# mLSTM of a two-layer trunk: own buffers for gate and second direction, its last products in other slots, unread products in another wait of PE

## The reference

```
u = layer_norm(x) * (1 + scale) + shift          # scale, shift, gate = silu(c) @ w_mod + b_mod
parts = split(u @ w_in)                          # q, k, v, z of branches A, B, C; B's o and gates; g_merge
# branch B, mLSTM, chunks of 128 tokens, forward and backward (d = 0, 1), 4 heads
s   = (q k^T) * exp(D - m)                       # "ST": scores, times decays
num = s v + w_inter * (C q)                      # "ND": numerator and, in column 129, denominator
den = sum(s) + w_inter * (n q)
h   = num / max(|den|, exp(-m))
C   = wc * C + (ws v)^T k                        # "CS": the state's update; "CX": the last state
y   = sigmoid(o) * (h_forward + h_backward)
merged += sigmoid(g) * ((y * silu(z)) @ w_branch)
x   = layer_norm(alpha * x + gate * (merged @ w_out)) * ln_g + ln_b
```

## Time and profile before

| | us |
|---|---|
| median of 3 runs | 1595.09 (1593.09 to 1595.38) |
| the profiled execution | 1593.39 |
| its span, first to last instruction | 1591.6 |
| PE busy in it | 1529.0 |
| mLSTM, from `scores(0)` to the gate projection, layer 0 / layer 1 | 644.09 to 666.75 / 1412.76 to 1437.35 |

### The profile page before, as it was taken

One profiled execution on the slowest core, in us unless ns is written; L12 is line 12 of the kernel. 1 busy time (PEld: TensorE's weight loads), 2 busy tenths in 40 slices (PEclk: granted clock), 3 DMA queues, 4 the chain that ended last, 5 costly groups with the idle time before them and its releaser, 6 DMA issues.

```text
span 1591.6 us, 22536 instructions
## 1 busy us (share of the span) xinstructions
PE 1529.0 (96%) x9059; PEld 1251.7 (79%) x9059; DVE 741.8 (47%) x1442; ACT 470.4 (30%) x1095; POOL 631.2 (40%) x504
## 2 busy tenths in 40 slices
PE   5999999999899999899999999999989999999997
PEld 4898788886688887788878977889758888777886
DVE  4496710646423332622497584125670136262256
ACT  1146710155410123411034485012571003232010
POOL 2561045600355353155772400555104554413562
PEclk9999999999999999999999999999999999999999
DMA  9220012327122222025440100222401221211421
GB/s 346 84 83 28 1 53 79 100 69 244 57 66 80 66 67 60 27 67 185 110 132 28 60 25 14 67 80 80 132 6 53 80 79 54 67 47 40 172 79 66
DMA packets 76135, 128.71 MB, mean 81 GB/s; under 512 B 16188, under 2 KB 20736, under 8 KB 76032
## 3 DMA queue, kind: packets, MB, share of 16 engines
q1 hardware_dynamic: 73792, 121.24, 24.7%
q10 hardware_dynamic: 2240, 6.03, 1.0%
HBM read 120.96 MB, written 6.30 MB: 80 GB/s over the span
## 4 chain that ended last, share of the span: by engine, by line
PE 79%; DVE 9%; POOL 3%; issue 3%; ACT 2%; DMA 2%; SPq 1%; POOLq 0%; DVEq 0%; ACTq 0%
PE pb L983 54%; PE pb L1126 5%; PE pb L1255 4%; PE pb L1008 2%; PE pb L1206 2%; PE pb L1169 2%; PE pb L931 2%; PE pb L1177 1%; PE pb L1299 1%; DMA stage<-in_w_mod 1%; DVE ks L2059 1%; PE pb L1436 1%; POOL slot_T L833 1%; DMA raw<-in_w_mod 1%; ACT pr L1704 1%
## 5 line engine op out<-in xcount | busy, mean ns | idle before, releaser
L983 PE MATMUL pb<-wsp,act_T 128*128 128x512 f32 x3060 | 714.5, 391 | 3.8 <-POOL wsp L833 2.1
L983 PEld LDWEIGHTS pb<-wsp,act_T 128*128 128x128 f32 x3060 | 570.9, 188 | 127.5 <-issue 7.8
L830 POOL CAST wsp<-raw 128x1024 fp32r<-128x1024 f32 x128 | 136.3, 1065 | 833.6 <-PE pb L983 664.6
L833 POOL TENSOR_TENSOR wsp<-raw,wsp 128x512 fp32r<-128x512 f32 x268 | 359.6, 1363 | 10.2
L983 PE MATMUL pb<-wsp,yT 128*128 128x512 f32 x720 | 165.7, 390 | 0.0
L983 PEld LDWEIGHTS pb<-wsp,yT 128*128 128x128 f32 x720 | 135.0, 188 | 27.9
L2516 DVE SCALAR_TENSOR_TENSOR mt<-tg,pb 128x512 f32<-128x512 f32 x40 | 27.4, 686 | 230.6 <-PE pb L983 229.7
L1854 ACT ACTIVATE tg<-pb 128x512 f32<-128x512 f32 x60 | 35.9, 599 | 289.6 <-PE pb L983 289.6
L1704 ACT ACTIVATE pr<-pb,nm 128x640 f32<-128x640 f32 (+2 forms) x128 | 91.3, 713 | 4.8 <-DVE nm L2200 4.8
L1206 PE MATMUL pb<-ident,pr 128*128 128x128 f32 x480 | 74.6, 277 | 7.2 <-ACT pT L1739 6.8
L2230 DVE TENSOR_SCALAR pr<-pr,rden 128x640 f32<-128x640 f32 (+2 forms) x128 | 69.8, 545 | 4.5
(11 more groups left out here) (281 smaller groups left out, 1961.7 us busy)
## 6 DMA issues: line engine op xcount, KB each, us to landing
raw<-in_w_in SPq DMA_DIRECT2D x112, 512.0 KB, 3.6
raw<-in_w_mod SPq DMA_DIRECT2D x32, 512.0 KB, 4.7
raw<-in_w_branch SPq DMA_DIRECT2D x24, 512.0 KB, 3.7
raw<-in_w_out SPq DMA_DIRECT2D x16, 512.0 KB, 3.7
stage<-in_w_mod SPq DMA_DIRECT2D x12, 512.0 KB, 11.7
raw<-in_w_in SPq DMA_DIRECT2D x16, 256.0 KB, 5.0
xh<-in_x_sample SPq DMA_DIRECT2D x6, 512.0 KB, 6.6
out<-xh ACTq DMA_DIRECT2D x5, 512.0 KB, 3.0
```

Source lines behind the costliest of these rows:

```text
L830: pool.tensor_copy(hi, raw[:, p % 3, :, 0:width]).then_inc(raw_hi, 1)
L833: ins = pool.tensor_tensor(lo[:, j, :], raw[:, p % 3, j, 0:width], hi[:, j, :].bitcast(F32), ALU.subtract)
L983: mm = pe.matmul(dst, lhs(a, k, t), w[:, wa, j, 0:width], start=(k == 0 and n == 0), stop=(i == count - 1 and j == 1 and n == 2))
```

## The change

Six edits. (1) At the start 6 unread products after i = 0 take the place of 8 after i = 1. (2) `ztmp` moves to addresses of its own, and the two waits of `decayed` on `zo` go; `finish` waits for `zo` instead. (3) `gate_zo` of tile 4 moves behind both denominators of chunk 0. (4) `t4` has two buffers, taken by turns; ACT's direction 1 waits for the read two chunks back. (5) The state updates CS 3, 4, 5 move from z's steps 17, 18, 19 to 16, 17, 18, so `scores(0)` follows z's last tile at once. (6) `hs` is turned in two groups: chunks 0 to 2 after part 0 of the gate projection, 3 and 4 after part 1.

```
-                     ("CS", (11, 13, 15, 17, 18, 19))):
+                     ("CS", (11, 13, 15, 16, 17, 18))):
...
-        t4 = at("t4", [P, HALF], F32, y_at + 18432)
...
-        ztmp = at("ztmp", [P, 2, HALF], F32, arena + 41056)
+        ztmp = at("ztmp", [P, 2, HALF], F32, arena + 79360)
+        t4 = at("t4", [P, 2, HALF], F32, arena + 83456)
...
+                        if i == 0:
+                            keep_busy(6)
                         if i == 1:
-                            keep_busy(8)
                             pe.wait_ge(xn_ready[0], T)
...
-                    if (i, t) == (0, T - 1):
-                        for c in range(T):
+                    if i < 2 and t == T - 1:
+                        for c in ((0, 1, 2), (3, 4))[i]:
...
-                            if d == 1 and c:
-                                act.wait_ge(t4_used[l], c)
+                            if d == 1 and c > 1:
+                                act.wait_ge(t4_used[l], c - 1)
                             for h in range(MH):
-                                dst = (hs[:, t, :], t4)[d][:, tile_cols(h)]
+                                dst = (hs[:, t, :], t4[:, c % 2, :])[d][:, tile_cols(h)]
...
-                        elif n != 1:
-                            dve.wait_ge(zo_ready[l], T - 1 if n == 0 else T)
...
-                        dve.tensor_tensor(hs[:, t, :], hs[:, t, :], t4[:, :], ALU.add).then_inc(t4_used[l], 1)
+                        dve.tensor_tensor(hs[:, t, :], hs[:, t, :], t4[:, c % 2, :], ALU.add).then_inc(t4_used[l], 1)
                         dve.wait_ge(t4_used[l], c + 1)
+                        dve.wait_ge(zo_ready[l], T if t == LT else t + 1)
...
                     for d in range(2):
                         decayed(0, d)
-                    gate_zo(T - 1)
...
                         if c:
                             finish(c - 1)
+                        else:
+                            gate_zo(T - 1)
```

## The result

| | before | after |
|---|---|---|
| median | 1594.38 us (1593.09 to 1595.38, 4 runs) | 1582.51 us (1581.72 to 1584.38, 4 runs) |
| the profiled execution, its span | 1593.39, 1591.6 | 1582.43, 1580.6 |
| start of the first projection | 34.14 | 32.16 |
| `scores(0)` to the gate projection, layer 0 / 1 | 22.66 / 24.59 | 20.12 / 20.11 |

The ratio is 0.9932, with a 95% interval of 0.992 to 0.9945: faster by 0.7%. The forecast was 1584.2 with a range of 1579.5 to 1589.0. Both profiled executions lie near their medians, so the 11.0 us between the spans can be followed along PE. How far after is ahead of before: 1.98 at the first projection, still 1.97 at `scores(0)` of layer 0, 4.51 at the gate projection behind its loop, 5.48 at the product with `yT`, 5.60 at `scores(0)` of layer 1, 10.08 behind that loop, 11.0 at the end.

The account below looks back on a forecast made before the run. PE, busy 1529.0 of 1591.6 us, was taken as the bound, so gains come from its waits, low-clock work or unread products. 0.82 + 2.52 + 4.45 + 1.40 = 9.19 off 1593.39 gave 1584.2 us, range 1579.5 to 1589.0.

Parts of the forecast that it names:

- Part 1: Start: 0.69 idle and four unread products put to use, 0.82 us if the clock rises at the same moment.
- first half of rival (a): Start: clock rises one slow stretch earlier, i = 2 starts 2.5 sooner, 1582.5 us; chance 0.17 for all of (a).
- second half of (a): End of layer 0's windowed attention: the 6.8 us clock fall may be spared, 1580.8 us; chance 0.17 for all of (a).
- Rival (c): Start: moved unread products fail, the clock rises only in the second burst; 1590.1 us, chance 0.06.
- Parts 2 to 5: mLSTM chunk loop, `scores(0)` to gate projection: 2.52 us less in layer 0, 4.45 in layer 1.
- The walk: Layer 0's chunk loop stepped wait by wait: first state product 1.34 us sooner, gate projection at 664.23 instead of 666.75.
- 0.3 or less: Sign of being right: in the chunk loop, L1437 to the next `hs` L1428 waits this instead of 1.75 us.
- POOL: Layer 0's loop: its split's L833 run to about 648.1, before `gate_zo` at 649.1; if hit, 0.1 late, sum unchanged.
- The rule on the port: DVE with two SBUF inputs and GpSimd reading SBUF contend; the later is blocked for the whole of the other.
- Layer 1: Its chunk loop: 2.52 as in layer 0 plus 1.93, the clock fall taken to be gone, 4.45 us.
- Rival (b): Chunk loop: another engine ends last or state updates delay `scores(1)`; half of 2.52 left per layer, 1588.7 us, chance 0.13.
- Part 6: Turning `hs`: the fourth chunk's wait for bank 1 goes, 0.70 us in each layer, 1.40 in all.

Follow-up runs that it names:

- `t4` alone: The kernel before with only a second `t4` buffer, taken by turns: 1591.33 us, ratio 0.9984.
- the gate alone: The kernel before with only `ztmp` in its own buffer and `gate_zo` of tile 4 behind chunk 0's denominators: 1587.33 us, ratio 0.9963.

## Why the prediction was right

The time came 1.7 us below the forecast: 1.16 of that at the start, 0.54 in turning `hs`; the two loops together hit their term.

- **Part 1** (0.82 forecast, 1.98 found). The place and the order of events were right; the sum rested on "if the clock rises at the same moment", and it did not. That was the first half of rival (a): 1.2 of the 2.0 us are luck. The same early rise was there twice with the old place, so it does not need the new one; the 0.82 for the same moment in both no pair of runs shows. The second half of (a) did not come: the fall at the end of the windowed attention is as long as before, 6.8 us. Rival (c), a rise only in the second burst, did not occur even without the burst.
- **Parts 2 to 5, layer 0** (2.52 forecast, 2.54 found). The walk named each wait and its size: 5.14 us to the first product with the state, and a last wait of 0.36 that is 0.31. The wait of 0.29 that is left in the first chunk was foreseen too ("0.3 or less"): it is the 0.60 + 1.19 that ACT needs from the denominator to PE. Off inside is only what each edit is worth: the step's new place is worth 1.34 by the walk, but 0.51 in the changed kernel, where edit (5) has moved POOL's pair 0.6 us back against `scores(0)`. The two dropped waits of `decayed` were said to cost nothing; one of them cost some 0.2. And edit (5) loses 0.10 by itself, as the walk has it (`scores(1)` 1.47 instead of 1.38 behind `scores(0)`).
- **POOL.** The forecast had its pair end at 648.1 and the new place of `gate_zo` at 649.1, 4.0 and 5.0 behind `scores(0)`. Measured: 646.14 and 647.05, that is 4.0 and 4.9 behind it. The rule on the port that it weighed holds, with one addition: what blocks is the instruction under way, not the pair.
- **Layer 1** (4.45 forecast, 4.48 found). That the fall of the clock goes with the long wait was taken as given; the run with `t4` alone, which kept the wait and the fall, and the one with the gate alone, which lost both, bear it out. Rival (b) is out: no other engine ended last, and the state updates pushed `scores(1)` back by only 0.10.
- **Part 6** (0.70 per layer forecast, 0.97 found, 0.99 by putting it back). The mechanism was right, the term was taken from the wait's row and is too small: by the starts the wait cost 1.12, with a second wait, of the fifth chunk, that no row shows. The second break cost 0.13, within the 0 to 0.15 allowed for.
- **The median.** I did not add the 1.7 us by which before's median lay above its profiled execution (1.0 with the fourth execution); after's lies 0.1 above its own. Had the 1.7 been added, the forecast would have been 1585.9.

## What to carry to other kernels

A chain of hand-made waits can be walked in advance: take the instruction that comes last at each wait, its latency to the next engine from a row (here 0.59 from DVE to ACT and 1.19 to PE), and step through; it hit a stretch of 20.1 us within 0.02. Terms that rest on the clock's moment are no such thing: give them both values. What a wait costs is read from starts, against the same group where it does not wait; the idle time in its row left out 0.4 of 1.1 us here. A wait that is bound by a bank is worth removing only if nobody then waits for the bank used in its place: the 1.1 us won by separate banks went into 1.7 us of waits one stage later, until the banks there were dealt out again.

## What the runs showed of the hardware

- The clock fell behind a wait of 1.75 us in the mLSTM loop of layer 1, in two traces out of two, and behind one of 1.70 to 2.06, followed by short products and a second wait of 0.29 to 1.64, at the end of layer 0's windowed attention, in eleven traces out of eleven; behind the same 1.75 in layer 0 it stayed, twice out of twice. Unread products in the waits of the windowed attention kept it at 1.00 in three out of three. The Trainium skill, page TensorE: Matmul & The Clock Gate, section Why this matters for your kernels, ties a fall to long idle gaps between bursts; here it fell behind waits below 2.1 us in some places, and the measurement decides.
- DVE, in an instruction with two SBUF inputs, and POOL hand the SBUF port over between instructions, even between two that POOL has back to back: DVE's step took 0.80 in place of 0.69 us and POOL's pair 2.95 in place of 2.50.
- A wait on PE shown as 0.69 us cost 1.12 us of the stretch: 0.93 between the starts, and 0.19 for a second wait that the rows hide.
- A wait of DVE for its own step cost some 0.2 us: the next instruction started 0.14 us behind the end of the step, and 0.07 ahead of it without the wait.
